# New orders around the norms, in the recurrent block and in the mixing block of a three-block transformer kernel

## The chip, the cores and the metric

The kernel runs on one core of a Trainium2 chip. The metric is the time of one execution on the device, in microseconds (us), as the median of several runs. The core's engines are TensorE (PE, matrix products; PEld is its weight load), VectorE (DVE), ScalarE (ACT), GpSimd (POOL) and SyncE (SP, which here only issues loads). They run apart from each other, each in the order of its own program, and wait for each other through counters (semaphores). On-chip memory is SBUF, and PE's results go to eight PSUM banks.

## The reference

The input is 256 tokens of 1024 features, all in fp32. Three blocks follow each other, with an RMS norm ahead of each projection: layer 0 (a gated linear recurrence and a SwiGLU FFN of 2816), layer 1 (stick-breaking attention and an FFN), and a mixing block (an attention with a relative bias, a gated recurrence in chunks, two gated outputs, an output projection and a gated embedding).

```python
u = einsum("bsd,de->bse", x, w_in) + b_in                  # recurrent block; x is normed
gate_branch, rec = u[..., :1024], causal_depthwise_conv(u[..., 1024:], conv_w, conv_b)
gl = einsum over 4 blocks of rec with gate_w, + gate_b
r_gate, i_gate = sigmoid(gl[0]), sigmoid(gl[1])
log_a = -8 * r_gate * softplus(-lam)
a = exp(log_a);  mult = sqrt(-expm1(2 * log_a))
h_t = a_t * h_(t-1) + mult_t * (i_gate_t * rec_t)
y = gelu(gate_branch) * h;  out = y @ w_out + b_out

h = h + swiglu_ffn(rms_norm(h))                            # silu(x w_g) * (x w_u), then w_out
```

## The kernel before

Every fp32 product is made of three products of a 32-bit type that PE takes at full rate: a value is split into a high part (`hi`) and what is left (`lo`), and `product_wide` (L500 to L508) and `product` (L444 to L450) add hi x hi, hi x lo and lo x hi. So each weight chunk passes through three steps. SP loads it into one of two `raw` buffers (1 MB, in two halves). ACT writes its high part `whi` (helper `split_part`, L982), and DVE its low part `wlo = raw - whi` (helper of the same name, L1497), each half by half, into one of four ring slots. PE then multiplies. A `raw` half is free again when its low part is made, and the load of the chunk two further on is issued then. `split(c)` does both halves of chunk c, and `ahead(c)` is `split(c + 3)`.

The chunks have numbers through the whole program: rec 0 to 3, gates_a 4, branch_a 5, gates_b 6, branch_b 7 to 9, lru_out 10 to 13, ffn_in0 from 14, and so on. The order of work on ACT and DVE is written out by hand as a list of calls.

In the recurrent block PE makes the rec branch, the gates and the gelu branch. ACT makes the sigmoids, `av = exp(log_a)`, a tanh of minus log_a (in `rg`) and its root (`gate_root`, L1118); since sqrt(1 - a^2) = sqrt(tanh) x (1 + a), DVE multiplies by `av + 1` in `scan(n)` (L1696 to L1705), then by the gated input `ig`, and runs the scan. n counts four groups of 256 channels. `output(n)` (L1711) multiplies by the gelu, which gives y; ACT makes `yhi` (L1137), DVE `ylo` (L1716). The output projection (`outputs_wide`, L524) takes chunks 10 and 11 whole, with y parts 0 and 1, and then chunks 12 and 13 in pieces, with parts 2 and 3. Chunk 12 completes the first half of the output's columns.

Around the norm: DVE adds the residual to `h` for the first half of the columns (`residual_wide(name, 0)`, L1572, one row for each 128 tokens). PE transposes that half (`transposes`, L510 and L515), in two groups with a piece of chunk 13 between them. ACT and DVE write the transposed values times the gain as `xhi` (L1014) and `xlo` (L1529), and the first FFN chunk starts with them. The second half follows behind the first FFN chunk (`late_transposes`). The same code serves attn_out (ahead of the second FFN), and the final projection out2.

In the mixing block, 24 chunks are made one after another, and the attention's small steps stand between them: scores on PE, `moba_max` (L1981), `moba_exp` (L1354), `moba_scale` (L1993), transposes (L820), `moba_copies` (L1362) and values (L831). Behind it stand the gated outputs up_a and up_b: ACT and DVE make `ybhi` and `yblo`, and DVE `ga` from the banks of up_a (L2192).

## Time and profile before

| what | value |
|---|---|
| median of 3 runs | 856.74 us (856.0 to 857.74) |
| the profiled execution | 855.25 us, of which the span of the trace is 853.5 |
| PE busy | 829.9 us (97%) |
| DVE busy | 571.7 us (67%) |
| ACT busy | 477.6 us (56%) |
| read from memory | 146.41 MB, 175 GB/s over the span |

Busy time is the sum over an engine's rows. PE's rows overlap, since a matmul starts before the last one has ended. The timeline gives each row its start, and in square brackets the idle time ahead of it and who ended it. The granted clock of PE (PEclk) is a share of its full rate of 2.4 GHz.

### The profile page before, as it was taken

Reading aid. Unit: us, or ns where it says so; the run is one execution under the profiler, and the core shown is the slowest. Engines: PE = TensorE matmul, PEld = TensorE weight load, DVE = VectorE, ACT = ScalarE, POOL = GpSimd, SP = SyncE. Lnnn points to the kernel's source line nnn. Section 1 sums busy time; section 2 is a strip of 40 time slices with the busy share of each in tenths; the row PEclk is TensorE's granted clock in tenths of the full one; section 3 lists DMA queues with packets and bytes.
Section 4 is the critical chain, followed back from the end, with each engine's and each line's share of the span. In section 5 each row is a group of like instructions: output and inputs, shape, how many; then the busy total and the mean of one; then the engine's idle time right before and its main releaser. Section 6 shows DMA issues by size and latency. Waiting matters only on the chain.

```text
span 853.5 us, 12729 instructions
## 1 busy us (share of the span) xinstructions
PE 829.9 (97%) x5093; PEld 736.3 (86%) x5093; DVE 571.7 (67%) x823; ACT 477.6 (56%) x676; POOL 2.1 (0%) x6
## 2 busy tenths in 40 slices
PE   6989899999999999999999999999999999999997
PEld 5988688888888899998788888888999999999886
DVE  5977866566544577775766665555657779887863
ACT  6699575444443566665754444435654756577441
POOL 0000000000000000000000000000000000000000
PEclk9999999999999999999999999999999999999999
DMA  8765748655566554443685565555554453443631
GB/s 278 212 184 176 242 143 281 206 182 179 196 195 191 157 178 128 140 148 104 208 253 177 176 193 183 191 187 181 173 173 138 140 168 117 132 148 119 207 119 50
DMA packets 124306, 148.31 MB, mean 174 GB/s; under 512 B 6216, under 2 KB 100952, under 8 KB 124120
## 3 DMA queue, kind: packets, MB, share of 16 engines
q1 hardware_dynamic: 122584, 144.73, 53.2%
q0 software_dynamic: 288, 1.05, 0.7%
q10 hardware_dynamic: 1376, 1.72, 0.6%
q8 instruction: 41, 0.67, 0.3%
q14 instruction: 17, 0.14, 0.1%
HBM read 146.41 MB, written 2.63 MB: 175 GB/s over the span
## 4 chain that ended last, share of the span: by engine, by line
PE 81%; DVE 8%; ACT 6%; DMA 3%; issue 2%; ACTq 0%; SPq 0%; DVEq 0%
PE bank L506 17%; PE bank L508 17%; PE bank L507 17%; PE bank L448 6%; PE bank L449 6%; PE bank L450 6%; DVE wlo L1497 3%; DMA raw<-in_lru_w_in 2%; PE bank L862 2%; PE bank L455 1%; ACT whi L982 1%; PE bank L456 1%; PE bank L457 1%; PE bank L656 1%; PE bank L515 1%
## 5 line engine op out<-in xcount | busy, mean ns | idle before, releaser
L1497 DVE TENSOR_TENSOR wlo<-raw,whi 128x1024 fp32r<-128x1024 f32 (+1 forms) x268 | 314.2, 1211 | 105.1 <-ACT whi L982 104.7
L982 ACT ACTIVATE whi<-raw 128x1024 fp32r<-128x1024 f32 (+1 forms) x268 | 268.9, 1048 | 179.8 <-PE bank L508 103.9
L448 PE MATMUL bank<-xhi,whi 128*128 128x256 f32 x576 | 165.2, 287 | 2.6 <-issue 2.6
L450 PE MATMUL bank<-xhi,wlo 128*128 128x256 f32 x576 | 162.9, 283 | 0.0
L449 PE MATMUL bank<-xlo,whi 128*128 128x256 f32 x576 | 162.9, 283 | 0.0
L506 PE MATMUL bank<-whi,xhi 128*128 128x512 f32 x384 | 151.9, 396 | 0.8 <-DVE xlo L1529 0.7
L508 PE MATMUL bank<-whi,xlo 128*128 128x512 f32 x384 | 149.9, 390 | 0.0
L507 PE MATMUL bank<-wlo,xhi 128*128 128x512 f32 x384 | 149.8, 390 | 0.0
L448 PEld LDWEIGHTS bank<-xhi,whi 128*128 128x128 f32 x576 | 110.3, 192 | 4.3 <-issue 3.7
L449 PEld LDWEIGHTS bank<-xlo,whi 128*128 128x128 f32 x576 | 110.4, 192 | 0.1
L450 PEld LDWEIGHTS bank<-xhi,wlo 128*128 128x128 f32 x576 | 110.4, 192 | 0.0
L506 PEld LDWEIGHTS bank<-whi,xhi 128*128 128x128 f32 x384 | 72.4, 189 | 15.5 <-issue 1.2
L508 PEld LDWEIGHTS bank<-whi,xlo 128*128 128x128 f32 x384 | 72.2, 188 | 15.3
L507 PEld LDWEIGHTS bank<-wlo,xhi 128*128 128x128 f32 x384 | 72.3, 188 | 14.4
L506 PE MATMUL bank<-whi,a_ghi 128*128 128x512 f32 x176 | 69.1, 392 | 0.0
L508 PE MATMUL bank<-whi,a_glo 128*128 128x512 f32 x176 | 68.6, 390 | 0.0
L507 PE MATMUL bank<-wlo,a_ghi 128*128 128x512 f32 x176 | 68.5, 389 | 0.0
L1213 ACT ACTIVATE a_sg<-bank,stat 128x256 f32<-128x256 f32 x44 | 18.5, 472 | 64.7 <-PE bank L508 64.7
L1777 DVE SCALAR_TENSOR_TENSOR a_gt<-bank,stat,a_sg 128x256 f32<-128x256 f32 x44 | 19.3, 479 | 47.0 <-ACT a_sg L1213 44.4
L508 PEld LDWEIGHTS bank<-whi,a_glo 128*128 128x128 f32 x176 | 33.0, 188 | 7.0
L507 PEld LDWEIGHTS bank<-wlo,a_ghi 128*128 128x128 f32 x176 | 33.1, 188 | 6.7
L506 PEld LDWEIGHTS bank<-whi,a_ghi 128*128 128x128 f32 x176 | 33.1, 188 | 6.7
(312 smaller groups left out, 1176.2 us busy)
## 6 DMA issues: line engine op xcount, KB each, us to landing
raw<-in_ffn_w_in SPq DMA_DIRECT2D x176, 256.0 KB, 3.7
raw<-in_w_in SPq DMA_DIRECT2D x48, 512.0 KB, 4.4
raw<-in_ffn_w_out SPq DMA_DIRECT2D x44, 512.0 KB, 4.2
raw<-in_attn_w_qkv SPq DMA_DIRECT2D x24, 512.0 KB, 4.5
raw<-in_lru_w_in SPq DMA_DIRECT2D x14, 512.0 KB, 5.2
raw<-in_lru_w_out SPq DMA_DIRECT2D x8, 512.0 KB, 4.9
raw<-in_attn_w_o SPq DMA_DIRECT2D x8, 512.0 KB, 3.9
raw<-in_w_out SPq DMA_DIRECT2D x8, 512.0 KB, 4.5
```

Of the source, the lines that this page charges most:

```text
L448: nc.tensor.matmul(dst, wh, hi, start=start, stop=False, skip_group_check=shared)
L449: nc.tensor.matmul(dst, wh, lo, start=False, stop=False, skip_group_check=shared)
L450: return nc.tensor.matmul(dst, wl, hi, start=False, stop=stop, skip_group_check=shared)
L455: nc.tensor.matmul(dst, hi, wh, start=start, stop=False)
L506: nc.tensor.matmul(dst, hi, wh, start=start, stop=False)
L507: nc.tensor.matmul(dst, hi, wl, start=False, stop=False)
L508: return nc.tensor.matmul(dst, lo, wh, start=False, stop=stop)
L862: last = nc.tensor.matmul(dst, k[:, u * P:(u + 1) * P], queries, start=True, stop=True)
L982: nc.scalar.activation(whi[:, c % RING, part], raw[:, c % RAWS, part], ACT.Copy).then_inc(hi_done, 1)
L1213: nc.scalar.activation(sg[:, q % 2, a, :], bank[(b0 + 2 * q + a) % 4][:, 0:S], ACT.Sigmoid, scale=stat[:, 10 * xn + 8 + a:10 * xn + 9 + a] ...
L1497: nc.vector.tensor_tensor(wlo[:, c % RING, part], raw[:, c % RAWS, part], whi[:, c % RING, part].bitcast(F32), ALU.subtract).then_inc(lo_d ...
L1777: marks.append(mark(nc.vector.scalar_tensor_tensor(out=gt[:, q % 2, a, :], in0=bank[(b0 + 2 * q + a) % 4][:, 0:S], scalar=tok(xn, a), in1= ...
```

## The change

In words, part by part:

- `transposes(xn, 0)` no longer waits for both residual rows. It goes token half by token half, and waits for the residual of each.
- Recurrent block: the multiply by `av + 1` is made on `ig` (new `decay_factor`), ahead of the wait for the root. DVE makes both the high and the low part of chunk 10 (new `split_alone`), ahead of the products of y; ACT's `split(10)` is gone, and ACT waits for DVE's high parts ahead of `split(11)`. `split(8)` goes ahead of `scan(1)`. The gated inputs 2 and 3 go ahead of `split(9)`. The halves of `split(11)` and `split(12)` are interleaved with scans and low parts of y. `split(13)` goes ahead of the low part of `p`.
- Norm behind lru_out: the halves of split(15) are put one ahead of the norm's `xhi`/`xlo` and one behind them, the residual goes ahead of both on DVE, and split(16) behind the norm's first half on ACT and the second residual on DVE. On attn_out the same, but ACT keeps its split whole ahead of `xhi`.
- Mixing block: ACT's `moba_copies(0)` and DVE's `moba_max(1)` go ahead of the split of their step. Behind it, `ybhi` goes ahead of `ahead(up_a + 1)`.

```diff
-            def transposes(xn, j):
-
-                for m in range(2):
-                    for a in range(2):
+            def transposes(xn, j, count=None):
+
+                for a in range(2):
+                    if count is not None:
+                        pe.wait_ge(banks_read, count + a + 1)
+                    for m in range(2):
...
-                pe.wait_ge(banks_read, b0 + 2 + 4)
-                transposes(xn, 0)
+                transposes(xn, 0, b0 + 4)
...
-            split(10)
             act.wait_ge(bkt_out, 16)
             y_hi_of(0)
             y_hi_of(1)
             gate_root(2)
+            act.wait_ge(hi_done, parts_done(10, 2))
             split(11)
...
             ahead(c0 + 1)
-            ahead(c0 + 2)
...
                 ahead(c0 + 3)
-                norm_hi(xn, 0)
-                norm_hi(xn, 1)
...
+            act.wait_ge(chunk_done, c0 + 2 + AHEAD + 1)
+            split_part(c0 + 2 + AHEAD, 0)
+            norm_hi(1, 0)
+            norm_hi(1, 1)
+            split_part(c0 + 2 + AHEAD, 1)
             norm_wide(1, c0, b0)
...
             ahead(c0 + 2)
+            norm_hi(3, 0)
+            norm_hi(3, 1)
             norm_wide(3, c0, b0)
...
             for c in range(24):
+                if c == 9:
+                    moba_copies(0)
                 ahead(c0 + c)
...
-            ahead(STAGES["up_a"][0] + 1)
             for n in range(2):
                 split_out(n, yb_ready, ke[:, n * PAIR:(n + 1) * PAIR], pair(ybhi, n), yb_hi)
+            ahead(STAGES["up_a"][0] + 1)
...
+            def decay_factor(n):
+
+                dve.wait_ge(a_ready, 8 * (n // 2) + 2 * (n % 2) + 2)
+                link(nc.vector.scalar_tensor_tensor(out=ig[:, n, :], in0=av[:, n, :], scalar=1.0, in1=ig[:, n, :],
+                                                    op0=ALU.add, op1=ALU.mult))
+
+            def split_alone(c):
+
+                dve.wait_ge(chunk_done, c + 1)
+                for n in range(2):
+                    part = slice(n * HALF, (n + 1) * HALF)
+                    dve.wait_ge(raw_full[c % RAWS][n], landed(c))
+                    nc.vector.tensor_copy(whi[:, c % RING, part], raw[:, c % RAWS, part]).then_inc(hi_done, 1)
+                    split_part(c, n)
...
             gated_input(0)
             gated_input(1)
+            decay_factor(0)
+            decay_factor(1)
             scan(0)
+            split(8)
             scan(1)
-            split(8)
-            split(9)
             gated_input(2)
             gated_input(3)
+            split(9)
+            split_alone(10)
+            decay_factor(2)
+            decay_factor(3)
             output(0)
             output(1)
-            split(10)
             output_lo(0)
             output_lo(1)
             scan(2)
-            split(11)
+            split_part(11, 0)
             scan(3)
+            split_part(11, 1)
             output(2)
             output(3)
-            split(12)
+            split_part(12, 0)
             output_lo(2)
             output_lo(3)
+            split_part(12, 1)
+            split(13)
...
+            residual_wide("lru_out", 0)
+            split_part(c0 + 2 + AHEAD, 0)
+            norm_lo(1, 0)
+            norm_lo(1, 1)
+            split_part(c0 + 2 + AHEAD, 1)
+            norm_end("lru_out", 1)
...
+                if c == 11:
+                    moba_max(1)
...
                 ahead(c0 + c)
```

What stands in a row on the engines, read from the two built programs. First DVE in the recurrent block, from the end of scan(0): `a_rg` and `a_ig` rows are the scan, `a_rc<-a_gel` is y. Before:

```order
L1699 SCALAR_TENSOR_TENSOR a_rg<-a_av_lru,a_rg 128x512
L1701 TENSOR_TENSOR a_rg<-a_rg,a_ig 128x512
L1704 SCALAR_TENSOR_TENSOR a_ig<-a_av_lru,a_rg 128x256 x2
L1497 TENSOR_TENSOR wlo<-raw,whi 128x1024 x4
L1694 TENSOR_TENSOR a_ig<-a_ig,a_rc 128x512 x2
L1711 TENSOR_TENSOR a_rc<-a_gel,a_ig 128x512 x2
L1497 TENSOR_TENSOR wlo<-raw,whi 128x1024 x2
L1716 TENSOR_TENSOR a_ylo<-a_rc,a_yhi 128x512 x2
```

And now:

```order
L1503 TENSOR_TENSOR wlo<-raw,whi 128x1024 x2
L1716 TENSOR_TENSOR a_rg<-a_rg,a_ig 128x512
L1719 SCALAR_TENSOR_TENSOR a_ig<-a_av_lru,a_rg 128x256 x2
L1696 TENSOR_TENSOR a_ig<-a_ig,a_rc 128x512 x2
L1503 TENSOR_TENSOR wlo<-raw,whi 128x1024 x2
L1710 CAST whi<-raw 128x1024
L1503 TENSOR_TENSOR wlo<-raw,whi 128x1024
L1710 CAST whi<-raw 128x1024
L1503 TENSOR_TENSOR wlo<-raw,whi 128x1024
L1701 SCALAR_TENSOR_TENSOR a_ig<-a_av_lru,a_ig 128x512 x2
L1726 TENSOR_TENSOR a_rc<-a_gel,a_ig 128x512 x2
L1731 TENSOR_TENSOR a_ylo<-a_rc,a_yhi 128x512 x2
```

The low part of chunk 8 stands ahead of scan(1), the high copies (CAST) and low parts of chunk 10 ahead of y, and the row `a_rg<-a_av_lru,a_rg` is gone from the scans, with `a_ig<-a_av_lru,a_ig` in its place.

Then DVE from y parts 2 and 3 to the norm; L1572 and L1578 are the residual, `xlo` the norm's low halves. Before:

```order
L1497 TENSOR_TENSOR wlo<-raw,whi 128x1024 x2
L1716 TENSOR_TENSOR a_ylo<-a_rc,a_yhi 128x512 x2
L1757 TENSOR_TENSOR a_plo<-bank,a_phi 128x512
L1497 TENSOR_TENSOR wlo<-raw,whi 128x1024 x6
L1572 TENSOR_TENSOR h<-bank,h 128x512 x2
L1497 TENSOR_TENSOR wlo<-raw,whi 128x1024 x2
L1529 SCALAR_TENSOR_TENSOR xlo<-bank,par,xhi 128x256 x4
L1572 TENSOR_TENSOR h<-bank,h 128x512 x2
L1538 TENSOR_TENSOR stat<-stat 128x2
L1529 SCALAR_TENSOR_TENSOR xlo<-bank,par,xhi 128x256 x4
```

And now:

```order
L1503 TENSOR_TENSOR wlo<-raw,whi 128x1024
L1731 TENSOR_TENSOR a_ylo<-a_rc,a_yhi 128x512 x2
L1503 TENSOR_TENSOR wlo<-raw,whi 128x1024 x3
L1779 TENSOR_TENSOR a_plo<-bank,a_phi 128x512
L1503 TENSOR_TENSOR wlo<-raw,whi 128x1024 x2
L1578 TENSOR_TENSOR h<-bank,h 128x512 x2
L1503 TENSOR_TENSOR wlo<-raw,whi 128x1024
L1535 SCALAR_TENSOR_TENSOR xlo<-bank,par,xhi 128x256 x4
L1503 TENSOR_TENSOR wlo<-raw,whi 128x1024
L1578 TENSOR_TENSOR h<-bank,h 128x512 x2
L1503 TENSOR_TENSOR wlo<-raw,whi 128x1024 x2
L1544 TENSOR_TENSOR stat<-stat 128x2
```

Ahead of the residual stand five `wlo` rows from the low parts of y on, where there were six, and the two of chunk 15 are behind it, one on each side of `xlo`.

Then ACT over the same stretch; `a_gel` is the gelu of parts 2 and 3, `sq` the norm's sums. Before:

```order
L1130 ACTIVATE a_gel<-bank,par 128x256 x4
L982 ACTIVATE whi<-raw 128x1024 x2
L1137 ACTIVATE a_yhi<-a_rc 128x512 x2
L1181 ACTIVATE a_phi<-bank 128x512
L982 ACTIVATE whi<-raw 128x1024 x8
L1014 ACTIVATE xhi<-bank,par 128x256 x4
L1025 ACTIVATE sq,stat<-h 128x512 x4
L1014 ACTIVATE xhi<-bank,par 128x256 x4
L982 ACTIVATE whi<-raw 128x1024 x2
```

And now:

```order
L1131 ACTIVATE a_gel<-bank,par 128x256 x4
L983 ACTIVATE whi<-raw 128x1024 x2
L1138 ACTIVATE a_yhi<-a_rc 128x512 x2
L1182 ACTIVATE a_phi<-bank 128x512
L983 ACTIVATE whi<-raw 128x1024 x5
L1015 ACTIVATE xhi<-bank,par 128x256 x4
L983 ACTIVATE whi<-raw 128x1024 x3
L1026 ACTIVATE sq,stat<-h 128x512 x4
L1015 ACTIVATE xhi<-bank,par 128x256 x4
L983 ACTIVATE whi<-raw 128x1024 x2
```

Of the eight high copies ahead of `xhi` three now stand behind it.

## Rows read from the trace of the kernel before

**Rows 1.** The page's first part: busy us, share of span, instructions.

```profile
PE 829.9 (97%) x5093; PEld 736.3 (86%) x5093; DVE 571.7 (67%) x823; ACT 477.6 (56%) x676; POOL 2.1 (0%) x6
```

**Rows 2.** Timeline of PE: start us, us, operation, shapes, [idle before <- what ended it].

```profile
63.97 0.36 PE L448 MATMUL bank<-xhi,whi 128*128 128x256 f32 x1 [2.34 <-issue]
...
77.41 0.47 PE L506 MATMUL bank<-whi,a_yhi 128*128 128x512 f32 x1 [1.27 <-DVE a_ylo L1716]
...
83.75 0.47 PE L506 MATMUL bank<-whi,a_yhi 128*128 128x512 f32 x1 [0.63 <-ACT a_gel L1130]
...
90.33 0.47 PE L506 MATMUL bank<-whi,a_yhi 128*128 128x512 f32 x1 [0.85 <-DVE a_ylo L1716]
...
99.50 0.39 PE L507 MATMUL bank<-wlo,a_yhi 128*128 128x512 f32 x1
...
99.72 0.39 PE L508 MATMUL bank<-whi,a_ylo 128*128 128x512 f32 x1
...
102.43 0.66 PE L515 MATMUL bank<-const,h 128*128 128x128 f32 x4 [2.32 <-DVE h L1572]
...
105.63 0.78 PE L506 MATMUL bank<-whi,xhi 128*128 128x512 f32 x1
...
412.44 0.47 PE L506 MATMUL bank<-whi,xhi 128*128 128x512 f32 x1 [0.66 <-DVE xlo L1529]
```

**Rows 3.** Stretches: us, busy PE, PEld, DVE, ACT, POOL, PEclk, DMA share, GB/s.

```profile
64.00:76.00 12.00, 12.00 (x100) 11.94 (x100) 7.62 (x9) 11.91 (x20) 0.00 (x0) 1.00 0.53 176
...
104.00:106.00 2.00, 2.00 (x8) 1.62 (x7) 1.45 (x3) 0.13 (x1) 0.00 (x0) 0.50 0.79 244
106.00:108.00 2.00, 2.00 (x8) 1.57 (x8) 1.11 (x3) 1.98 (x6) 0.00 (x0) 0.76 0.90 286
```

**Rows 4.** Waits of PE, whole run: us in total, times, longest.

```profile
PE bank L831 <- ACT a_probs_t L1362: 1.2, 1, 1.2
...
PE bank L820 <- DVE a_probs L1993: 0.6, 1, 0.6
...
PE bank L448 <- DVE a_ga L2192: 0.4, 1, 0.4
```

**Rows 5.** Timeline of DVE in the recurrent block.

```profile
59.89 0.69 DVE L1699 SCALAR_TENSOR_TENSOR a_rg<-a_av_lru,a_rg 128x512 f32<-128x512 f32 x1
...
62.64 4.63 DVE L1497 TENSOR_TENSOR wlo<-raw,whi 128x1024 fp32r<-128x1024 f32 x4
...
72.69 1.35 DVE L1711 TENSOR_TENSOR a_rc<-a_gel,a_ig 128x512 f32<-128x512 f32 x2 [4.09 <-ACT a_gel L1130]
...
76.58 1.28 DVE L1716 TENSOR_TENSOR a_ylo<-a_rc,a_yhi 128x512 fp32r<-128x512 f32 x2
```

**Rows 6.** Timeline of ACT in the recurrent block.

```profile
73.20 2.02 ACT L982 ACTIVATE whi<-raw 128x1024 fp32r<-128x1024 f32 x2
...
75.09 1.16 ACT L1137 ACTIVATE a_yhi<-a_rc 128x512 fp32r<-128x512 f32 x2
```

**Rows 7.** Loads of chunks 10 and 11 (tile raw, stretch 60 to 72).

```profile
DMA to landing us min/median/max: 3.5/5.7/6.0
```

**Rows 8.** Timeline of DVE, a one-source operation of 128x1024.

```profile
658.33 0.69 DVE L2002 TENSOR_SCALAR a_log_f_b<-a_fb 128x1024 f32<-128x1024 f32 x1
```

**Rows 9.** Timeline of DVE at the end of the output projection.

```profile
99.95 1.23 DVE L1497 TENSOR_TENSOR wlo<-raw,whi 128x1024 fp32r<-128x1024 f32 x1 [0.68 <-ACT whi L982]
101.09 1.28 DVE L1572 TENSOR_TENSOR h<-bank,h 128x512 f32<-128x512 f32 x2
```

**Rows 10.** Timeline of ACT at the end of attn_out.

```profile
407.91 2.01 ACT L982 ACTIVATE whi<-raw 128x1024 fp32r<-128x1024 f32 x2 [1.31 <-PE bank L508]
```

**Rows 11.** Timelines of ACT and DVE in the mixing block.

```profile
662.18 2.01 ACT L982 ACTIVATE whi<-raw 128x1024 fp32r<-128x1024 f32 x2
...
678.09 2.35 DVE L1497 TENSOR_TENSOR wlo<-raw,whi 128x1024 fp32r<-128x1024 f32 x2
```

**Rows 12.** Timeline of ACT behind the mixing block.

```profile
780.54 2.00 ACT L982 ACTIVATE whi<-raw 128x1024 fp32r<-128x1024 f32 x2
```

More of the change, by code:

```diff
@@ L1407, in _ @@
                 if c == 9:
-                    moba_copies(0)
                     decay_ln()
@@ L1940, in _ @@
             outputs(GROUPS - 1)
-            ahead(c0a + 2)
-            norm_wide("attn_out", 3)
+            split_part(c0a + 2 + AHEAD, 0)
+            residual_wide("attn_out", 0)
+            split_part(c0a + 2 + AHEAD, 1)
+            norm_lo(3, 0)
+            norm_lo(3, 1)
+            norm_end("attn_out", 3)
             ffn(1)
@@ L2102, in _ @@
                 if c == 11:
-                    moba_max(1)
                     silu(8, qb, 0, 1)
```

16 lines of the change are left out of this document (4 added, 12 removed).

## The prediction

> **What bounds the kernel now.** I read three views: the page's first part, then the timeline of TensorE (PE), then the rows of VectorE (DVE) and ScalarE (ACT) just ahead of each wait that PE shows. PE is busy 97% of an 853.5 us span [rows 1], so nothing can be won except where PE waits or runs at the low clock; work taken from DVE or ACT is worth nothing unless it ends such a wait. In the timeline PE waits five times in the recurrent block: 2.34 us ahead of chunk 8 (at 63.97), 1.27 ahead of the output projection (77.41), 0.63 and 0.85 inside it (83.75, 90.33), and 2.32 ahead of the first transposes of the norm (102.43) [rows 2]. The last wait is followed by a stretch at the low clock: the granted clock, 1.00 before (2.4 GHz), is 0.50 (1.2 GHz) and 0.76 in two stretches of 2 us [rows 3]. Behind that PE runs without a wait until 412.44 (0.66), and then the mixing block has 1.2 and 0.6, and its end 0.4 [rows 2, 4]. Where PE does not wait, a row reaches about 0.17 into the next one (0.39 long, the next starts 0.22 later), so a wait that goes gives back its length and 0.17 more.
>
> **Chunk 8 (wait of 2.34).** PE needs the low part `wlo` of chunk 8. DVE makes it from 62.64, behind scan(1), which runs from 59.89 [rows 5]: 2.75 us. The change puts split(8) ahead of scan(1) and takes the factor multiply (0.69, the row at 59.89) out of scan(0) too, so `wlo` 8 starts near 59.2; its halves, 4.63 / 4 = 1.16 each, are ready at 60.4 and 61.5. PE comes for them at 61.5 (63.97 less 2.34 and 0.17) and for the second half 1.4 later. The wait goes: -2.5. The factor multiplies of 0 and 1 now stand ahead of scan(0), where DVE waits for ACT's root anyway; they cost nothing.
>
> **Ahead of the output projection (1.27).** PE, 2.5 earlier, would arrive at 73.5. It waits for y_lo(0): gelu, product, high copy, low part. Before, ACT made the two high halves of chunk 10 between gelu and the high copies (73.20, 2.02 long), and DVE the low halves right ahead of `ylo` (76.58) [rows 5, 6]. Now DVE makes both parts of chunk 10 earlier, in the 4.09 us that it stood idle before 72.69 [rows 5]. Does it fit? Split(9) now ends near 67.1 (scan(1) to 63.4, two gated inputs 1.4, `wlo` 9 2.3). Chunk 10's load is issued when `wlo` 8 is done, 60.4 and 61.5, and takes 3.5 to 6.0 [rows 7]: there by 66.4 and 67.5. The cost of DVE's high copy of 128x1024 (new; no row has a one-source operation that writes the high type) lies between a tensor_scalar of that size, 0.69, and a two-source one, 1.23 [rows 8, 9]; I take 0.69, its nearest kin in sources and memory. Then 2 x (0.69 + 1.15) + two factors of 0.7 = 5.1, from 67.1 to 72.2: just ahead of the product at 72.69. With 1.23 it is 73.3 and y comes 0.6 late; an edge below nothing has no reason, since the product waits for gelu. So the product stays at 72.69 (0.68 each), the high copies (0.6 each) at 73.4 and 74.05, y_lo(0) is done at 74.7, and PE starts at 74.9 instead of 77.41: -2.5, with 1.3 of waiting still there. The Trainium skill, page "VectorE: DVE Perf Modes", section on the perf-mode tier table, gives a one-source copy from SBUF to SBUF in fp32 double rate and a two-source one none; that the row at 658.33 agrees (half of a two-source row) says nothing of this output type, and by the page the copy takes the lower end.
>
> **Chunk 11 (0.63).** It waits for gelu(2) and (3) to empty the banks. On ACT these stand behind the high copies, the root's table and root, split(11) and gelu's table. The second high copy ended at 76.25 (75.09 + 1.16 [rows 6]) and now ends at 74.65: the whole chain moves 1.6. PE starts chunk 11 at 82.2 instead of 83.75: only -1.6, and its wait grows to about 1.6. A new wait on ACT for DVE's high parts of chunk 10 (ready about 70) stands there ahead of split(11) at 77; nothing is held up.
>
> **Chunk 12 (0.85).** It waited for the third y_lo, which stood behind both low halves of chunk 12. DVE's row from 76.6 is now scan(2), `wlo` 11 first half, scan(3), second half, products 2 and 3, `wlo` 12 first half, y_lo(2), y_lo(3); with 2.0 for a scan, 1.15 for a half and 0.6 for a 512 row it reaches y_lo(2) at 85.9. PE comes at 82.2 + 5.6 = 87.8. No wait; -2.5 at this point (90.33 before).
>
> **Residual and transposes (2.32).** Before, the residual add (101.09) stood on DVE behind `wlo` 15 (99.95), whose load came late [rows 9]. Now both halves of `wlo` 15 stand behind it, and the transposes wait for each half of the residual apart. PE needs 9.6 from 90.33 to 99.94, so it reaches the transposes at 97.4; chunk 12 ends six matmuls earlier, 96.1, and two residual rows of 0.64 end at 97.4. The load of chunk 14, ahead of it, is issued at 85.3 and 87.7 and with 6.0 its low part is done by 96.0. The wait goes: transposes at 97.5 instead of 102.43, -5.0. With no wait I expect no fall of the clock: transposes and six matmuls then take 2.2 (0.41 + 6 x 0.23 + 0.41) and not 3.2, so the FFN starts at 99.7 instead of 105.63, -5.9; the clock of 0.76 in the stretch from 106 gives 0.5 more (2 x 0.24). **Block: -6.4.** What moves back: the second half of split(15) and split(16) come after the norm's halves, on both engines, and loads 17 and 18 start later. PE wants chunk 17 at 117; it has landed by about 109.
>
> **attn_out (0.66).** `xlo` waited for `xhi` behind ACT's high copy of 2.01 at 407.91 [rows 10], which now follows it: -0.7. The transposes' finer waits: between 0 and one residual half, 0.64, in three places; I take 0.2 in all (of short waits that no answer lists).
>
> **Mixing block.** moba_copies(0) goes ahead of the high copy at 662.18 (2.01 [rows 11]): the copies move 1.9 earlier and the wait of 1.2 goes, -1.3. Behind it moba_max(1) goes ahead of the `wlo` at 678.09 (2.35) [rows 11], and so exp, scale and transposes could come 2.3 earlier; but PE arrives 1.3 earlier, and ahead of the scale now stand that `wlo`, two silus (1.4) and the values (0.9): scale starts at about 685.0 rather than 686.55. Of the old 0.6 about 0.4 stays: -0.2. End: the high parts of y_b stood behind the high copy at 780.54 (2.00 [rows 12]) and now come first; `a_ga` follows 1.9 earlier and the wait of 0.4 goes with its tail, -0.5.
>
> **Sum.** 6.4 + 0.7 + 0.2 + 1.3 + 0.2 + 0.5 = 9.3. The profiled execution took 855.25 (span 853.5), 1.5 under the median of the runs, 856.74: its successor would be 845.9, and the median 847.4.
>
> **Rivals.**
> (a) DVE becomes late in the block: a copy of 1.23 (+0.6) and landings at 6.0 or more, and then the residual is behind again by up to 1.5 with part of the slow clock after it (1.5 by the two clock rows: 2 x 0.50 + 2 x 0.24). Time 847.4 + 0.6 + 1.5 + 1.0 = 850.5. For it: DVE has 0.5 of slack before the product; before, DMA was busy all the time from 99 on. Against: every other margin is over 1.
> (b) The clock falls elsewhere. The two waits that stay, 1.3 and 1.6 with 5.5 of work between, are shorter than the 2.34 ahead of 63.97, behind which the clock stayed at 1.00 [rows 3]; against it the 2.32 behind which it fell. Price as in those rows, 1.5: 848.9. The Trainium skill, page "TensorE: Matmul & The Clock Gate", section on what you observe and what happens, says that the monitor runs freely and the point of a change differs from run to run; the two rows agree, like waits with unlike ends.
> (c) Slower: the clock falls at the first remaining wait and stays low. A wide matmul starts 0.23 after the last at full clock; at half it is 0.43, 0.2 more. 47 such matmuls use up 9.3; if all 96 of the projection ran so, +19.2 less about 3.6 of waits covered: 863. Against it: the low stretch of before ended within 5 us.
> (d) The moves don't reach PE: the order on the engines shows them, but the waits had other ends than shown, and only chunk 8 and the residual pay: 856.74 - 5.0 = 851.7.
>
> **Chances.** Forecast (845.4 to 848.8) 0.62; (a) 0.14; (b) 0.10; more than forecast (the chunk 11 wait shorter, full 0.6 in the mixing block, 844.5) 0.06; (d) 0.05; (c) 0.03. The range 844.3 to 850.9 holds the first four. A measurement of this kernel tells 0.2% from no change: faster 0.96, within 0.01, slower 0.03.
>
> **What will show it.** PE's timeline: no wait ahead of chunk 8 (near 61.5), first projection row at 74.9, chunk 11 at 82.2 behind `a_gel`, no wait at 87.8, transposes near 97.5, clock 1.00 throughout, FFN at 99.7. DVE's high copy near 0.69. No wait of PE on `a_probs_t`, about 0.4 on `a_probs`, none on `a_ga`. Wrong would be: DVE's copy over 1.3, a residual that starts over 1 us after chunk 12, a clock under 0.9 between 62 and 110, or a wait on `wlo` in the first FFN chunks.

## The result and the profile after

| | before | after |
|---|---|---|
| median of the runs | 856.75 us (4 runs, 856.0 to 857.74) | 847.01 us (4 runs, 846.38 to 847.37) |
| the profiled execution | 855.25, span 853.5 | 846.38, span 844.6 |

The ratio is 0.9878, with a 95% interval of 0.9863 to 0.9893: 9.7 us less. The prediction was 847.4, with a range of 844.3 to 850.9. Two statements ahead are not right: `rg` holds a tanh of minus half of log_a, not of minus log_a; and on attn_out DVE keeps the first low half of its chunk ahead of the residual and puts the second between the residual and `xlo`, so only the halves behind lru_out stand as told. No number of the prediction hangs on either.

The page's first part, after (busy us, share of the span, instructions), to set beside [rows 1]:

```profile
PE 827.6 (98%) x5093; PEld 735.4 (87%) x5093; DVE 573.3 (68%) x825; ACT 475.5 (56%) x674; POOL 2.1 (0%) x6
```

DVE does 1.6 us more and ACT 2.1 less, but neither bounds the kernel: the 8.9 us by which the span shrank are waits of PE that went, and matmuls that now run at full clock (PE is busy for 2.3 us less). The waits of PE over the whole run, after (us in total, times, longest), to set beside [rows 4]:

```profile
PE bank L506 <- DVE a_ylo L1731: 1.8, 1, 1.8
PE bank L506 <- ACT a_gel L1131: 1.5, 1, 1.5
PE bank L448 <- issue: 0.2, 1, 0.2
PE bank L821 <- DVE a_probs L2022: 0.2, 1, 0.2
```

The two waits of the mixing block and the one at its end (1.2, 0.6 and 0.4) shrank to a single 0.2. PE's timeline, after, at the places of [rows 2]: chunk 8, the projection, chunk 11, chunk 12, the transposes, the first FFN matmul, and the first FFN matmul behind attn_out:

```profile
61.78 0.28 PE L448 MATMUL bank<-xhi,whi 128*128 128x256 f32 x1
...
75.65 0.47 PE L506 MATMUL bank<-whi,a_yhi 128*128 128x512 f32 x1 [1.76 <-DVE a_ylo L1731]
...
82.88 0.47 PE L506 MATMUL bank<-whi,a_yhi 128*128 128x512 f32 x1 [1.51 <-ACT a_gel L1131]
...
88.41 0.39 PE L506 MATMUL bank<-whi,a_yhi 128*128 128x512 f32 x1
...
97.94 0.69 PE L517 MATMUL bank<-const,h 128*128 128x128 f32 x4
...
100.56 0.47 PE L506 MATMUL bank<-whi,xhi 128*128 128x512 f32 x1
...
405.87 0.47 PE L506 MATMUL bank<-whi,xhi 128*128 128x512 f32 x1
```

Of the five waits in the recurrent block two are left. The stretches around the transposes, after (us, busy PE, PEld, DVE, ACT, POOL, PEclk, DMA share, GB/s), to set beside [rows 3]:

```profile
98.00:100.00 2.00, 2.00 (x13) 1.58 (x12) 1.73 (x4) 0.84 (x2) 0.00 (x0) 1.00 0.15 51
100.00:102.00 2.00, 1.90 (x11) 1.45 (x9) 1.05 (x4) 1.51 (x3) 0.00 (x0) 1.00 0.69 233
102.00:104.00 2.00, 2.00 (x10) 1.66 (x9) 1.93 (x3) 2.00 (x3) 0.00 (x0) 1.00 0.09 29
```

The clock stays at 1.00 (2.4 GHz) here and everywhere else in the block. DVE in the recurrent block, after, to set beside [rows 5] and [rows 9]:

```profile
59.83 2.36 DVE L1503 TENSOR_TENSOR wlo<-raw,whi 128x1024 fp32r<-128x1024 f32 x2
...
67.86 0.69 DVE L1710 CAST whi<-raw 128x1024 fp32r<-128x1024 f32 x1
68.58 1.23 DVE L1503 TENSOR_TENSOR wlo<-raw,whi 128x1024 fp32r<-128x1024 f32 x1
69.72 0.69 DVE L1710 CAST whi<-raw 128x1024 fp32r<-128x1024 f32 x1
...
71.59 1.41 DVE L1701 SCALAR_TENSOR_TENSOR a_ig<-a_av_lru,a_ig 128x512 f32<-128x512 f32 x2
73.37 1.35 DVE L1726 TENSOR_TENSOR a_rc<-a_gel,a_ig 128x512 f32<-128x512 f32 x2 [0.36 <-ACT a_gel L1131]
...
96.84 1.29 DVE L1578 TENSOR_TENSOR h<-bank,h 128x512 f32<-128x512 f32 x2 [2.45 <-PE bank L508]
98.05 1.22 DVE L1503 TENSOR_TENSOR wlo<-raw,whi 128x1024 fp32r<-128x1024 f32 x1
```

The new high copy takes 0.69. All of DVE's new work fits ahead of the product, with 0.36 left. The residual (96.84) now waits for PE and not for a load: it follows chunk 12 at once, and `wlo` 15 stands behind it.

**A fixed point to measure from.** The two profiles don't agree on when the recurrent block gets going. ACT in the second half of the gates, before:

```profile
50.68 1.06 ACT L982 ACTIVATE whi<-raw 128x1024 fp32r<-128x1024 f32 x1 [1.02 <-DMA raw<-in_lru_w_in]
...
60.75 1.57 ACT L1099 ACTIVATE a_rg<-bank,par 128x256 f32<-128x256 f32 x4
```

and after:

```profile
51.35 1.06 ACT L983 ACTIVATE whi<-raw 128x1024 fp32r<-128x1024 f32 x1 [0.96 <-DMA raw<-in_lru_w_in]
...
61.42 1.57 ACT L1100 ACTIVATE a_rg<-bank,par 128x256 f32<-128x256 f32 x4
```

A load of chunk 7 landed 0.67 later, and ACT's row of the second sigmoids, which I call Z, is exactly 0.67 later too. Z moved between 60.75 and 63.02 over the 14 profiles of this study, and except in `e8_decay_early` no edit changes what it waits for. The distance from the first sigmoids of the gates to Z is 15.89 where ACT does not wait for a load between them, and up to 17.73 (in `e1_chunk8_late`) where it does; how the start before that moves was not followed to its cause. From Z on, the rows of one kernel keep their places: in the second profile of the changed kernel, below, each place stands within 0.06 of where the first has it, and the two profiles of another kernel (`e4_gelu_early` and `e4_again`) differ by 0.08 at most. So I compare places by their distance from Z:

| us behind Z | before | after | moved | forecast |
|---|---|---|---|---|
| projection starts | 16.66 | 14.23 | -2.43 | -2.5 |
| chunk 11 | 23.00 | 21.46 | -1.54 | -1.6 |
| chunk 12 | 29.58 | 26.99 | -2.59 | -2.5 |
| transposes | 41.68 | 36.52 | -5.16 | -5.0 |
| first FFN matmul | 44.88 | 39.14 | -5.74 | -5.9 |
| one `L506` row further on | 46.28 | 39.90 | -6.38 | -6.4 |
| PE's last matmul | 787.78 | 778.23 | -9.55 | -9.3 |

### The profile page after: what moved, and what is told of

Its sections match the earlier page's. It is cut to its first block, busy times and chain, and to the rows that moved or that the text cites. A ratio compares the mean times of both kernels' runs of the same rounds, so it can differ in the third digit from the quotient of the medians.

```text
span 844.6 us, 12734 instructions
## 1 busy us (share of the span) xinstructions
PE 827.6 (98%) x5093; PEld 735.4 (87%) x5093; DVE 573.3 (68%) x825; ACT 475.5 (56%) x674; POOL 2.1 (0%) x6
## 3 DMA queue, kind: packets, MB, share of 16 engines
q10 hardware_dynamic: 1376, 1.72, 0.7%
## 4 chain that ended last, share of the span: by engine, by line
PE 85%; DVE 6%; ACT 5%; DMA 3%; issue 1%; SPq 0%; ACTq 0%; DVEq 0%
PE bank L506 18%; PE bank L508 18%; PE bank L507 18%; PE bank L448 7%; PE bank L449 6%; PE bank L450 6%; DVE wlo L1503 2%; DMA raw<-in_lru_w_in 2%; PE bank L863 2%; PE bank L455 1%; PE bank L457 1%; PE bank L456 1%; ACT whi L983 1%; PE bank L657 1%; PE bank L517 1%
## 5 line engine op out<-in xcount | busy, mean ns | idle before, releaser
L506 PE MATMUL bank<-whi,xhi 128*128 128x512 f32 x384 | 151.6, 395 | 0.3
L506 PEld LDWEIGHTS bank<-whi,xhi 128*128 128x128 f32 x384 | 72.1, 188 | 15.2 <-issue 0.9
L506 PE MATMUL bank<-whi,a_ghi 128*128 128x512 f32 x176 | 69.1, 392 | 0.0
L506 PEld LDWEIGHTS bank<-whi,a_ghi 128*128 128x128 f32 x176 | 33.0, 188 | 6.7
```

What stands on the lines that cost most here:

```text
L506: nc.tensor.matmul(dst, hi, wh, start=start, stop=False)
```

## The experiments

Each is an edit of the changed kernel, unless said otherwise. `after_again`, `e4_gelu_early`, `e4_again` and `e8_decay_early` have four executions each, whose median the table gives; the others are one profiled execution, and since Z alone moves those by a microsecond or two, what is said of them rests on distances from Z. `e4_gelu_early` and `e4_again` are one kernel. The kernel before, beside them on the same chips, took 856.84 (7 runs, `e1` to `e4_gelu_early`), 857.78 (7 runs, `after_again`, `e4_again`, `e8`, `m1`) and 857.15 (one run, `e5`, `m2`, `e6`, `e9`).

| run | time | Z | projection | chunk 11 | chunk 12 | FFN | last matmul |
|---|---|---|---|---|---|---|---|
| before | 856.75 | 60.75 | 16.66 | 23.00 | 29.58 | 44.88 | 787.78 |
| after | 847.01 | 61.42 | 14.23 | 21.46 | 26.99 | 39.14 | 778.23 |
| after_again | 847.00 | 61.07 | 14.23 | 21.45 | 26.99 | 39.14 | 778.29 |
| e1_chunk8_late | 847.99 | 63.02 | 14.22 | 21.45 | 26.98 | 39.12 | 778.24 |
| e2_act_makes_10 | 849.72 | 61.33 | 16.66 | 25.04 | 30.48 | 42.62 | 781.66 |
| e3_norm_order_back | 849.75 | 62.12 | 14.23 | 21.46 | 27.02 | 41.87 | 780.90 |
| e9_factor_in_scan | 847.80 | 62.66 | 14.17 | 21.46 | 27.03 | 39.29 | 778.39 |
| e5_norm_order_only | 852.89 | 61.81 | 16.72 | 23.01 | 29.60 | 42.08 | 784.35 |
| m1_max_late | 848.84 | 62.30 | 14.23 | 21.46 | 27.02 | 39.17 | 779.82 |
| m2_copies_late | 848.07 | 62.77 | 14.24 | 21.47 | 27.00 | 39.15 | 778.56 |
| e6_small_parts_back | 848.23 | 62.02 | 14.23 | 21.46 | 26.99 | 39.35 | 779.49 |
| e4_gelu_early | 847.35 | 62.55 | 14.24 | 19.78 | 25.58 | 37.95 | 777.05 |
| e4_again | 845.14 | 61.12 | 14.23 | 19.77 | 25.58 | 37.93 | 776.97 |
| e8_decay_early | 844.85 | 60.92 | 14.23 | 19.76 | 25.57 | 37.92 | 777.09 |

### Chunk 8's low part behind scan(1) again

```diff
             scan(0)
-            split(8)
             scan(1)
+            split(8)
             gated_input(2)
```

> The kernel after, with split(8) on VectorE behind scan(1) again. TensorE gets chunk 8 about 2.0 us later (near 63.8 instead of 61.78). My sum booked 2.5 us for this part. Theory 1 (the terms add): the first FFN matmul comes 2.0 later, 102.6 instead of 100.56, and the run takes 2.0 more. Theory 2 (behind the recurrent block the chain of ScalarE sets the projection and its second chunk, and TensorE only arrives earlier to wait): the wait ahead of the projection shrinks from 1.76 to under 0.3, the chunk that waits for the gelu still starts near 82.9, and the run takes 0.2 to 0.9 more, the latter if the later load of chunk 10 delays VectorE's high copy.

The wait ahead of chunk 8 is back, and the one ahead of the projection has nearly gone (PE's timeline):

```profile
64.78 0.36 PE L448 MATMUL bank<-xhi,whi 128*128 128x256 f32 x1 [2.47 <-issue]
...
77.24 0.47 PE L506 MATMUL bank<-whi,a_yhi 128*128 128x512 f32 x1 [0.28 <-DVE a_ylo L1731]
```

The first wait is 2.47, but the projection starts 14.22 behind Z, as without it (14.23), and so does all the rest; this one execution took 1.61 more than the profiled one of the changed kernel (847.99 to 846.38), and its Z is 1.60 later. Theory 2 is what happened. Moving `split(8)` is worth nothing in this kernel: it makes PE arrive 1.5 earlier (the wait ahead of the projection is 1.76 instead of 0.28) at a place where it has to wait for y anyway. What sets the projection is ACT's row of work from Z to the gelu, and the short chain behind it. The clock stayed at 1.00 in the stretches of 2 us from 62 to 70, though this wait is longer than the 2.32 of before, behind which it fell.

### ACT makes chunk 10's high part again

```diff
             split(9)
-            split_alone(10)
             decay_factor(2)
...
             output(1)
+            split(10)
             output_lo(0)
...
             branch_gelu(c0, 1)
+            split(10)
             act.wait_ge(bkt_out, 16)
...
-            act.wait_ge(hi_done, parts_done(10, 2))
```

> The kernel after, with the high part of chunk 10 made by ScalarE between the gelu and the high copies of y, and its low part by VectorE behind y, as in the kernel before. Theory: the high copies come 1.9 later, so the projection starts near 78.2 instead of 75.65, its second chunk near 84.7 instead of 82.88, and the FFN 1.9 later. Rival: the copy on VectorE gained nothing, since y waited for the gelu anyway, under 0.5. The wait ahead of the projection grows to about 4.3 us; if a long wait alone brings the clock down, the granted clock behind it is under 1.00 and 1.5 more is lost.

The projection starts 16.66 behind Z, where it started before the change, 2.43 later than in the changed kernel. PE, which comes early, waits 3.91, and then the clock falls. PE's timeline and the stretches behind it:

```profile
77.99 0.76 PE L506 MATMUL bank<-whi,a_yhi 128*128 128x512 f32 x1 [3.91 <-DVE a_ylo L1731]
```

```profile
78.00:80.00 2.00, 2.00 (x5) 1.61 (x6) 1.61 (x3) 1.99 (x4) 0.00 (x0) 0.50 0.78 268
80.00:82.00 2.00, 2.00 (x7) 1.51 (x6) 1.97 (x4) 1.98 (x3) 0.00 (x0) 0.50 0.42 159
82.00:84.00 2.00, 2.00 (x6) 1.61 (x5) 1.94 (x4) 1.99 (x6) 0.00 (x0) 0.50 0.28 61
```

Six us at 0.50 (1.2 GHz). Chunk 10 takes 8.38 (16.66 to 25.04) where its work takes 5.72 at full clock (14.23 to 21.46, less the wait of 1.51): 2.7 more. There is no wait left ahead of chunk 11; at full clock there would have been one, since before, with the same order on ACT, chunk 11 came at 23.00. So some 2.0 of the 2.7 (25.04 less 23.00) reached chunk 11. At the last matmul 3.43 are lost in all, so that DVE's share of chunk 10 without the clock is worth about 1.4 (an estimate, 3.43 less 2.0). Expected was an FFN 1.9 later and, if the clock fell, 1.5 more; it was 3.48 later. The edit moves two things back, ACT's high part and the place of DVE's low part, and does not separate them: the last to end ahead of `ylo` was the low part (DVE's row of 74.88, 2.36 long), 0.4 behind the high copies of y (ACT's row of 75.66, 1.16 long).

### The order around the norm as before

```diff
-            act.wait_ge(chunk_done, c0 + 2 + AHEAD + 1)
-            split_part(c0 + 2 + AHEAD, 0)
+            ahead(c0 + 2)
+            ahead(c0 + 3)
             norm_hi(1, 0)
             norm_hi(1, 1)
-            split_part(c0 + 2 + AHEAD, 1)
...
+            ahead(c0 + 2)
             residual_wide("lru_out", 0)
-            split_part(c0 + 2 + AHEAD, 0)
+            ahead(c0 + 3)
             norm_lo(1, 0)
             norm_lo(1, 1)
-            split_part(c0 + 2 + AHEAD, 1)
```

> The kernel after, with the order around the norm behind lru_out as before: both halves of split(15) ahead of the residual and of the norm's halves, split(16) next (the transposes still wait for each half of the residual apart). Theory: the residual stands behind the second low half of chunk 15, whose load lands near 97.4, so it starts near 99.7 instead of 96.84 and TensorE waits about 2.4 ahead of the transposes; with the low clock behind it (0.5 in one stretch of 2 us), the FFN starts 3.3 to 4 later. Rival: the earlier low parts alone have already brought the load of chunk 15 forward enough, and under 1.0 is lost. Clock: if it falls as before, a wait of this length ahead of transposes suffices; if it stays at 1.00, the FFN starts only 2.5 later.

DVE at the end of the projection, and PE:

```profile
97.01 2.58 DVE L1506 TENSOR_TENSOR wlo<-raw,whi 128x1024 fp32r<-128x1024 f32 x2 [1.48 <-ACT whi L983]
99.51 1.28 DVE L1581 TENSOR_TENSOR h<-bank,h 128x512 f32<-128x512 f32 x2
100.71 2.35 DVE L1506 TENSOR_TENSOR wlo<-raw,whi 128x1024 fp32r<-128x1024 f32 x2
102.97 0.87 DVE L1538 SCALAR_TENSOR_TENSOR xlo<-bank,par,xhi 128x256 fp32r<-128x256 f32 x2
```

```profile
100.25 0.44 PE L517 MATMUL bank<-const,h 128*128 128x128 f32 x2 [1.42 <-DVE h L1581]
...
103.99 0.47 PE L506 MATMUL bank<-whi,xhi 128*128 128x512 f32 x1 [0.88 <-DVE xlo L1538]
```

Both halves of `wlo` 15 are ahead of the residual again, and `wlo` 16 ahead of `xlo`. PE waits twice, 1.42 and 0.88, and the FFN starts 2.73 later behind Z (2.67 at the last matmul). The clock stays at 1.00 behind both. Expected were one wait of 2.4 and 3.3 to 4 lost with the low clock, or 2.5 without it; the second is near.

### The order around the norm alone, on the kernel before

The same edit the other way round, on the kernel before (ACT and DVE of the norm behind lru_out; nothing else).

```diff
             ahead(STAGES["lru_out"][0] + 1)
-            ahead(STAGES["lru_out"][0] + 2)
             dve.wait_ge(bout_in, 32)
-            norm_wide("lru_out", 1)
+            residual_wide("lru_out", 0)
+            split_part(c0 + 2 + AHEAD, 0)
+            norm_lo(1, 0)
+            norm_lo(1, 1)
+            split_part(c0 + 2 + AHEAD, 1)
+            residual_wide("lru_out", 1)
+            ahead(c0 + 3)
...
```

> The kernel before, with one part of the change: the order around the norm behind lru_out (residual ahead of both low parts of chunk 15, one high and low half of chunk 15 on each side of the norm's halves, split(16) behind). The transposes still wait for both residual rows. Theory: the wait of 2.32 ahead of the transposes shrinks to under 0.6 (it may keep a second residual row), the clock does not fall there, and from the FFN on TensorE stands 3.3 to 3.9 earlier than before, while the four waits ahead of it stay (2.3, 1.3, 0.6, 0.9). Rival: without the earlier work in the block the load of chunk 14 holds the residual back, since its low part stands ahead of it, and under 2 is won.

The wait of 2.32 ahead of the transposes has gone, and the clock at 102 to 106 is 1.00. The FFN's row that stood 46.28 behind Z stands at 42.86, and the last matmul is 3.43 earlier: of the block's 6.38, the norm's order alone is worth 3.4. That is more than the 2.67 of the last experiment: there the order of before cost two waits, on the kernel before it cost a wait and the low clock behind it. In this execution the clock fell elsewhere, behind the wait ahead of chunk 8 (stretches of PE):

```profile
65.04 0.36 PE L448 MATMUL bank<-xhi,whi 128*128 128x256 f32 x1 [3.17 <-issue]
```

```profile
66.00:68.00 2.00, 2.00 (x13) 2.00 (x13) 2.00 (x3) 1.98 (x2) 0.00 (x0) 0.60 0.80 266
68.00:70.00 2.00, 2.00 (x12) 2.00 (x12) 1.64 (x3) 1.96 (x6) 0.00 (x0) 0.55 0.85 248
```

It cost nothing: PE came to the projection without a wait, in place of one of 1.27, and the projection started 16.72 behind Z (16.66 before). The waits ahead of chunks 11 and 12 stayed at 0.63 and 0.86, as expected.

### The factor multiply back in the scan

```diff
-            decay_factor(0)
-            decay_factor(1)
...
-            decay_factor(2)
-            decay_factor(3)
...
                 dve.wait_ge(mult_ready, n + 1)
+                link(nc.vector.scalar_tensor_tensor(out=rg[:, n, :], in0=av[:, n, :], scalar=1.0, in1=rg[:, n, :],
+                                                    op0=ALU.add, op1=ALU.mult))
                 link(nc.vector.tensor_tensor(rg[:, n, :], rg[:, n, :], ig[:, n, :], ALU.mult))
```

> The kernel after, with the factor (av + 1) multiplied in the scan, behind the root, as before. Theory: VectorE's row is as long as before up to the product, since two factors of 0.7 move into scans 0 and 1 and two leave from ahead of the product, so the projection starts at the same distance of 14.2 behind the second sigmoids; scans 2 and 3 grow by 0.7 each, y_lo(2) comes near the time at which TensorE wants it for chunk 12, so 0 to 0.5 is lost. Rival: the factor is what brought the projection forward, and 0.7 to 1.4 is lost at its start.

The projection starts at 14.17, chunk 11 at 21.46, the FFN 0.15 later and the last matmul 0.16 later. Moving four multiplies of 0.7 out of the scans, 2.8 us of DVE's work in the place where it seemed tightest, is worth 0.16.

### Two parts of the mixing block

`moba_max(1)` behind the split of its step again:

```diff
-                if c == 11:
-                    moba_max(1)
...
                 if c == 11:
+                    moba_max(1)
                     silu(8, qb, 0, 1)
```

> The kernel after, with moba_max(1) behind VectorE's split of its step again. Theory: TensorE still comes 1.3 earlier by the copies' move, so it waits for the scaled probabilities about 1.9 instead of 0.17, and from there on stands 1.6 to 1.8 later: undoing this small part costs more than both parts of the mixing block together brought, 1.5. Rival: the two parts are worth 1.3 and 0.2 as in my sum, and 0.2 is lost.

and `moba_copies(0)` behind the split again:

```diff
-                if c == 9:
-                    moba_copies(0)
                 ahead(c0 + c)
...
                 if c == 9:
+                    moba_copies(0)
                     decay_ln()
```

> The kernel after, with moba_copies(0) behind ScalarE's split of its step again. Theory: TensorE waits 1.2 for the copies again and then, coming later, no longer 0.17 for the scaled probabilities: 1.1 to 1.3 more from there on. With the run that undid moba_max alone (1.6 more) and the whole part, worth 1.5, this says that neither of the two is worth its share alone. Rival: nothing is lost, because the second wait takes it all.

Undoing the first costs 1.59 at the last matmul, near the 1.6 to 1.8 expected; undoing the second costs 0.33, and the 1.1 to 1.3 expected of it were wrong. PE in the mixing block, in `m1`:

```profile
681.81 1.92 PE L821 MATMUL bank<-const,a_probs 128*128 128x128 f32 x12 [1.72 <-DVE a_probs L2022]
```

and in `m2`, where the old wait is back, but the one ahead of the transposes has gone:

```profile
660.81 0.66 PE L832 MATMUL bank<-a_probs_t,a_mv 128*64 128x256 f32 x4 [1.21 <-ACT a_probs_t L1367]
...
681.45 1.47 PE L821 MATMUL bank<-const,a_probs 128*128 128x128 f32 x12
```

DVE's scale before, in the changed kernel and in `m2`:

```profile
686.79 1.92 DVE L1993 TENSOR_SCALAR a_probs<-a_probs,small 128x256 f32<-128x256 f32 x8
```

```profile
678.72 1.93 DVE L2022 TENSOR_SCALAR a_probs<-a_probs,small 128x256 f32<-128x256 f32 x8
```

```profile
680.09 1.93 DVE L2021 TENSOR_SCALAR a_probs<-a_probs,small 128x256 f32<-128x256 f32 x8
```

The last two are 617.30 and 617.32 behind Z: the copies don't move the scale. With the copies early and the max late (`m1`), PE comes early only to wait 1.72 for the scale instead of the 0.64 of before, and wins nothing. With the max early and the copies late (`m2`), PE comes to the transposes 0.77 later behind Z than in the changed kernel, but goes through them in 1.47 where there it takes 1.92 at the pace of the scale, so that 0.33 of the 0.77 is left. It is the move of `moba_max`, which brings the scale forward, that pays. In `m1` the clock fell as well, in the recurrent block, behind a wait of 2.33 ahead of the projection (76.53):

```profile
76.00:78.00 2.00, 1.47 (x4) 1.21 (x5) 0.99 (x2) 1.97 (x3) 0.00 (x0) 0.60 0.13 49
78.00:80.00 2.00, 2.00 (x7) 1.57 (x6) 1.73 (x3) 2.00 (x4) 0.00 (x0) 0.54 0.00 0
```

and it cost nothing, as the wait of 1.5 ahead of chunk 11 took it up (21.46 as ever).

### The small parts

The transposes wait for both residual rows again, and `ybhi` stands behind the split:

```diff
-                transposes(xn, 0, b0 + 4)
+                pe.wait_ge(banks_read, b0 + 2 + 4)
+                transposes(xn, 0)
...
+            ahead(STAGES["up_a"][0] + 1)
             for n in range(2):
                 split_out(n, yb_ready, ke[:, n * PAIR:(n + 1) * PAIR], pair(ybhi, n), yb_hi)
-            ahead(STAGES["up_a"][0] + 1)
```

> The kernel after, with two small parts undone at places far apart: the transposes wait for both residual rows again (three places), and the high parts of y_b stand behind ScalarE's split again. Theory: 0.2 to 0.6 more at the first transposes behind lru_out, up to 0.3 at attn_out and at out2, and 0.5 at the first matmul that waits for a_ga. Rival for the transposes: nothing, since TensorE comes later than the second row.

The last matmul is 1.26 later. By place (the steps in PE's distance from Z against the changed kernel's, each read some rows behind the place, where it has settled): 0.22 behind lru_out, 0.23 behind attn_out, 0.62 at `a_ga`, where the wait of 0.39 is back, and 0.22 at out2; between the places the distance drifts by 0.05 in all. The finer waits so give about 0.67 in three places, not 0.2.

### What still stands ahead of the projection and chunk 11

Both waits that are left hang on ACT. The gelus of parts 2 and 3 need only their banks, and yet stood behind the root's table and root, `split(11)` and the gelu's table. So: gelus first, and DVE makes chunk 11 as it makes chunk 10.

```diff
             y_hi_of(1)
-            gate_root(2)
-            act.wait_ge(hi_done, parts_done(10, 2))
-            split(11)
-            nc.scalar.preload_act_table_set("gelu_apprx_tanh_and_others")
             branch_gelu(c0 + 1, 2)
             branch_gelu(c0 + 2, 3)
+            gate_root(2)
+            act.wait_ge(hi_done, parts_done(11, 2))
             split(12)
...
+            split_alone(11)
             scan(2)
-            split_part(11, 0)
             scan(3)
-            split_part(11, 1)
```

> A new version on top of the kernel after: ScalarE makes gelu 2 and 3 right behind the high copies of y 0 and 1, ahead of the root, while the gelu table is still loaded (one table load less), and VectorE makes both parts of chunk 11, in the 1.25 us in which it waited for the root and on. Theory: TensorE's wait of 1.51 for the gelu goes, the second chunk starts near 81.2 instead of 82.88, the next near 86.8 to 87.2 instead of 88.41, and the run takes 1.2 to 1.7 less. Rival: VectorE is the bound (two more high copies of 0.69, and scans 2 and 3 start at 79.7 instead of 77.4), y parts 2 and 3 come late, and chunk 12 waits: under 0.5 less, or no gain.

Its median showed no gain at first, so it and the changed kernel were timed once more on one chip. First the changed kernel:

> The kernel after, unchanged, on the chip of the next two, to compare medians. Theory: 847.0 within 0.7. In the profile the first matmul of the projection stands 14.2 us behind the start of the second gates' sigmoids on ScalarE, and the first FFN matmul 39.1 behind it, wherever that start falls; before it was 16.7 and 44.9. If the terms add up on TensorE instead, these distances change when the sigmoids start elsewhere.

Then the new version:

> The version with gelu 2 and 3 ahead of the root and both parts of chunk 11 made by VectorE, measured again beside the kernel after on one chip, since its profile showed the FFN 37.9 us behind the sigmoids instead of 39.1, but a median of 847.35. Theory: the 1.2 us are real and the difference came from the start (ScalarE's chain began 1.1 later in that run): 0.9 to 1.2 less than the kernel after in the median. Rival: no gain in the median, since what is won in the block is lost by later loads.

The gelus follow the high copies of y at once, and one change of ACT's table goes. ACT, in `e4_again`:

```profile
73.85 1.23 ACT L1138 ACTIVATE a_yhi<-a_rc 128x512 fp32r<-128x512 f32 x2 [0.16 <-DVE a_rc L1724]
74.99 1.55 ACT L1131 ACTIVATE a_gel<-bank,par 128x256 f32<-128x256 f32 x4
76.56 1.28 ACT L1123 ACT_TABLE_LOAD   x1
```

PE no longer waits ahead of chunk 11, which comes 1.69 earlier behind Z; a wait of 0.21 for `ylo` appears ahead of chunk 12:

```profile
75.35 0.47 PE L506 MATMUL bank<-whi,a_yhi 128*128 128x512 f32 x1 [1.50 <-DVE a_ylo L1729]
...
86.70 0.47 PE L506 MATMUL bank<-whi,a_yhi 128*128 128x512 f32 x1 [0.21 <-DVE a_ylo L1729]
```

At the last matmul it is 1.18 (`e4_gelu_early`) and 1.26 (`e4_again`) earlier than in the first profile of the changed kernel. The four times of `e4_gelu_early` gave 847.35 (846.32 to 848.84; ratio to before 0.9889, 0.9865 to 0.9913), no better than the changed kernel, as its Z was late (62.55 in the profile). Timed again beside the changed kernel on one chip, it took 845.14 (844.84 to 845.49; 0.9855, 0.9839 to 0.9872), and the changed kernel 847.00 (846.11 to 848.36; 0.9877, 0.9862 to 0.9892). The intervals overlap; all four times of the one lie below all four of the other on that chip, but not in the first measurement. What is shown is the distance, twice, at the lower end of the 1.2 to 1.7 expected; the medians are a weaker sign of it.

Last, on top of it, ACT's chain from gates_a to Z. There ACT waits for the second half of chunk 7 (the row at 51.35 above), while `exp(log_a)` behind it needs nothing that is not there.

```diff
-            split(7)
+            act.wait_ge(chunk_done, 8)
+            split_part(7, 0)
             gate_decay(0)
+            split_part(7, 1)
             gate_root(0)
...
-            split(7)
+            split_part(7, 0)
             gated_input(0)
             gated_input(1)
             decay_factor(0)
             decay_factor(1)
+            split_part(7, 1)
             scan(0)
```

> On top of the last version: ScalarE makes the first decay (exp and tanh of parts 0 and 1, 3.4 us) ahead of the second high half of chunk 7, for whose load it stood idle 0.96 us in the kernel after (1.0 before, 1.2 in other runs), and VectorE the gated inputs and factors 0 and 1 ahead of its second low half. Theory: from the gates on ScalarE's chain sets the start of the projection, so the idle time goes from the end: 0.9 to 1.3 less than the last version, about 845.0, with no wait of TensorE for chunk 7 or 8. Rival: TensorE's own work sets the projection, and only the wait ahead of it changes; or chunk 7's second half comes late (it is wanted near 57.2) and TensorE waits up to 1 us there.

```profile
49.91 1.04 ACT L983 ACTIVATE whi<-raw 128x1024 fp32r<-128x1024 f32 x1
50.86 1.69 ACT L1110 ACTIVATE a_av_lru<-a_rg,small 128x256 f32<-128x256 f32 x4
52.58 1.71 ACT L1116 ACTIVATE a_rg<-a_rg,small 128x256 f32<-128x256 f32 x4
54.20 1.04 ACT L983 ACTIVATE whi<-raw 128x1024 fp32r<-128x1024 f32 x1
```

ACT doesn't wait here, and from the first sigmoids of gates_a to Z it needs 15.89 (45.03 to 60.92), where the changed kernel needs 16.96 (44.46 to 61.42). The wait is gone, but `m2` shows the same 15.89 (46.88 to 62.77) without this edit, since its ACT came too late to wait for that load. PE's wait ahead of the projection falls to 0.66. The edit moves Z itself, so the distance would have to be taken from PE's first product matmul: to the last one it is 825.87 and 825.76 in the two profiles of the changed kernel, 824.96 and 824.36 in the two of `e4_gelu_early`, and 823.64 here. One kernel's two profiles differ by 0.60 in it, so the 0.72 to `e4_again` is no proof. The median, 844.85 (844.49 to 847.16; ratio 0.9856, 0.9840 to 0.9873), can't be told from the 845.14 beside it, and the 0.9 to 1.3 expected are not shown. In the medians `e4_again` and this kernel lie 1.9 and 2.2 us below the changed kernel; the intervals of all three overlap.

## Why the prediction was right, and where it was not

**Places.** Each place of the block was 0.3 to 0.9 later in the profile than the number given (75.65 for 74.9, 82.88 for 82.2, 100.56 for 99.7). 0.67 of it is the later Z; by distance from Z (forecast place less 60.75) they are right within 0.23; only chunk 8, which doesn't hang on Z, stands apart. So the argument from a timeline row by row held: each duration was that of a row of before, the new copy's that of its nearest row.

**The copy on DVE.** 0.69, the lower end, as taken from the one-source row of 658.33 [rows 8]. The slack ahead of the product was given as 0.5 and was 0.36. The Trainium skill, page "VectorE: DVE Perf Modes", section on the perf-mode tier table, gives a one-source fp32 copy within SBUF double rate and a two-source operation none: the trace agrees in the main for this output type too, 0.69 for the copy and 1.23, 1.8 times as long, for the two-source `wlo` of the same size.

**Chunk 8 (-2.5).** PE did come earlier (61.78 for 63.97), but the step reads as if it paid, and rival (d) even counts on it for its 851.7. `e1` shows that alone it is worth 0.0. The sum didn't suffer, as the steps were places of PE and not amounts to be added. The wait ahead of the projection was forecast as 1.3 and was 1.76: PE came to it 0.4 later than forecast (73.89 for 73.5), and the projection, which hangs on Z, started 0.75 later. Where that wait is shorter, as in `e8` (0.66), the move may pay; no run tried it.

**Chunk 10, 11, 12.** Right: -2.43, -1.54, -2.59 for -2.5, -1.6, -2.5. `e2` shows that all 2.43 of the projection's move hang on DVE's share of chunk 10. The order of the halves of chunks 11 and 12, which the prediction counts on for chunk 12, was not undone alone. `e9` shows that taking the multiply out of the scans, of which the prediction made one of two reasons for chunk 8, does next to nothing.

**Residual and transposes.** Right: the wait went, and the low clock behind it (-5.16 for -5.0; with what the clock gives back -6.38 for -6.4). From the transposes to the FFN it took 2.62 and not 2.2. Behind lru_out the finer waits were counted at nothing or a share of 0.2, and `e6` measures 0.22 there: in the block one error hides part of the other.

**attn_out and the finer waits.** The first FFN matmul behind attn_out came 0.86 earlier on top of the block (412.44 to 405.87 is 6.57, and 0.67 for Z, less 6.38), and 0.81 are left by the end of that FFN, for 0.7; by `e6` 0.23 of it is the finer wait, so that about 0.6 remain for the move of ACT's copy and DVE's halves. No run undid those alone. The term of 0.2 for the finer waits was too small: about 0.67 in three places. The prediction put their bound at one residual row, 0.64, each; a third of that in each place is what they gave.

**Mixing block.** Sum right (1.54 for 1.5), shares wrong. The forecast place of the scale was right: 1.55 earlier, and measured 1.55 (626.04 behind Z before, 686.79 less 60.75, and 617.30 after, less the 7.19 that PE had won just ahead of the block). But the prediction gave 1.3 to the copies and left 0.2 to the max. With the copies moved and not the max (`m1`) the block wins nothing, 1.54 less 1.59; with the max and not the copies (`m2`) 1.54 less 0.33, 1.21. The step that failed is "the wait of 1.2 goes, -1.3": it counts a removed wait of PE as a gain without asking what sets PE's next meeting with DVE, which is the scale. The wait on `a_probs` that was to stay at 0.4 was 0.17, since PE came to it 1.07 earlier and not 1.3.

**`a_ga` and out2.** -0.62 for -0.5; out2 gave 0.19, by `e6` (0.22) all of it the finer wait.

**Sum.** 6.38 + 0.81 + 1.54 + 0.62 + 0.19 = 9.54, for 9.3 (at the last matmul 9.55); the later Z took 0.67 back. The measured span shrank by 8.9, and the medians by 9.7: which Z an execution has moves it by more than the error of the sum, so that a median within 0.4 of the forecast is in part luck.

**Rivals.** (a) fell: copy at 0.69, and DVE idle for 2.45 ahead of the residual (the loads of before, which it takes as busy all the time from 99 on, were done by 109). (b) is real, but not in the changed kernel's profiles: behind waits of 1.76 and 1.51 the clock stayed; in `m1`, with a wait of 2.33 at the same place, it fell. Its price was given as 1.5; there it was 0, and in `e2` about 2.0: what counts is whether a wait stands behind to take it up. (c) was not seen: the longest low stretch, in `e2`, ended within 7 us. (d) fell: the projection, chunk 11, the mixing block and `a_ga` moved too. What was not weighed is the landing of the early loads, by which Z, and all behind it, moves by up to 2.3.

## What to carry to other kernels

A wait that vanishes is worth only what the next meeting with a later engine lets through: follow the late engine's own chain to the next place, and cost the place, not the wait. Before two profiles are compared, find the last row that hangs on something outside the change (here a load) and measure from there; effects from about 0.1 us on can then be read from single executions whose times differ by 2, since here two profiles of one kernel agreed within 0.06 and 0.08. Where one engine stands ahead of a wait with work of another kind (a high copy, a change of table), look first for idle time on the other engine that can do it.
